# A hybrid decoder layer on one core: weights laid out in the order of their use, and loaded in longer runs and larger chunks

## The reference, cut to what matters

```
proj = xn @ w_in                      # 1024 x 11264, then w_a, w_b, w_o
...
logits = xt @ w_router ; top 4 of 32 experts per token, gates = softmax(top)
h = xb @ w1[e] + b1[e]                # 1024 x 2048 per expert
gate = min(h[:, :1024], 7) ; up = clip(h[:, 1024:], -7, 7)
y = ((up + 1) * gate * sigmoid(1.702 * gate)) @ w2[e] + b2[e]   # 1024 x 1024
```

## Time and profile before

| what | value |
|---|---|
| three runs | 1490.82, 1487.87, 1491.01 us; median 1490.82 |
| the profiled execution | span 1490.0 us, 0.8 us below the median; the page gives no time beyond the span |
| TensorE matmuls busy | 1384.2 us, 93% |
| VectorE, ScalarE, GpSimd busy | 25%, 15%, 6% |
| bytes moved | 518.50 MB (10^6 bytes), mean 348 GB/s over the span |
| loads of the ring | SP's queue, 469.10 MB |

### The profile page before, as it was taken

The page is one execution under the profiler, slowest core; times in us unless marked ns, Lnnn a source line. Parts: engine busy times, 40 slices in busy tenths (PEclk is TensorE's granted clock), DMA queues, the critical chain, the costliest instruction groups (busy, mean ns, idle before and its releaser), DMA issues.

```text
span 1490.0 us, 18645 instructions
## 1 busy us (share of the span) xinstructions
PE 1384.2 (93%) x7365; PEld 705.1 (47%) x7365; DVE 374.4 (25%) x677; ACT 228.6 (15%) x340; POOL 96.3 (6%) x160
## 2 busy tenths in 40 slices
PE   7999999999999998998999989989999899899896
PEld 6667668778887433333333333333323333333231
DVE  3224332532501322122122121221221212211123
ACT  1122232211000411111001011110110111110102
POOL 1022222210000200000000000000000000000000
PEclk9999999999999999999999999999999999999999
DMA  9887868876334479999999999999999999999995
GB/s 351 311 292 282 282 238 292 273 252 208 135 134 175 165 290 420 415 420 417 415 422 415 418 420 415 420 416 416 421 415 419 418 415 422 415 417 420 415 420 214
DMA packets 119137, 518.50 MB, mean 348 GB/s; under 512 B 9240, under 2 KB 9512, under 8 KB 86303
## 3 DMA queue, kind: packets, MB, share of 16 engines
q1 hardware_dynamic: 104442, 469.10, 78.4%
q0 software_dynamic: 12720, 45.14, 9.0%
q10 hardware_dynamic: 1940, 3.78, 0.7%
HBM read 496.35 MB, written 21.67 MB: 348 GB/s over the span
## 4 chain that ended last, share of the span: by engine, by line
PE 76%; DMA 12%; SPq 4%; DVE 3%; ACT 2%; issue 1%; POOL 0%; DVEq 0%; ACTq 0%; POOLq 0%
PE bank L1522 25%; PE bank L1258 18%; PE bank L1557 11%; PE bank L1568 6%; DMA ring<-in_w_e 6%; SPq L520 4%; DMA out_ret_sample<-arena 4%; PE bank L1502 3%; PE bank L1301 3%; PE bank L1395 2%; PE bank L1520 1%; ACT arena L848 1%; PE bank L1360 1%; DVE arena L1209 1%; DVE hx L1213 1%
## 5 line engine op out<-in xcount | busy, mean ns | idle before, releaser
L1522 PE MATMUL bank<-ring,arena 128*64 128x512 f32 x2048 | 444.8, 592 | 0.3 <-ACT arena L839 0.3
L1258 PE MATMUL bank<-arena,ring 128*128 128x264 f32 x1536 | 350.3, 388 | 0.0
L1258 PEld LDWEIGHTS bank<-arena,ring 128*128 128x128 f32 x1536 | 290.2, 190 | 53.4 <-issue 5.0
L1522 PEld LDWEIGHTS bank<-ring,arena 128*64 128x64 f32 x2048 | 143.8, 137 | 283.3 <-issue 277.8
L1557 PE MATMUL bank<-ring,arena 128*64 128x512 f32 x1024 | 227.2, 593 | 5.0 <-DMA ring<-in_w_e 5.0
L1557 PEld LDWEIGHTS bank<-ring,arena 128*64 128x64 f32 x1024 | 70.9, 137 | 139.9 <-issue 117.5
L1198 DVE TENSOR_SCALAR arena<-bank 128x512 f32<-128x512 f32 x32 | 22.1, 692 | 397.0 <-PE bank L1522 397.0
L1568 PE MATMUL bank<-arena 128*128 128x512 f32 (+1 forms) x192 | 91.3, 610 | 12.6 <-DVE arena L1209 12.6
L1502 PE MATMUL bank<-arena 128*128 128x128 bf16 x768 | 60.0, 236 | 29.6 <-DVE arena L1190 29.5
L1209 DVE COPY arena<-bank 64x512 f32<-64x512 f32 x32 | 21.9, 683 | 236.1 <-PE bank L1557 236.1
L1502 PEld LDWEIGHTS bank<-arena 128*128 128x128 bf16 x768 | 54.6, 107 | 44.7 <-issue 44.7
(11 more groups left out here) (198 smaller groups left out, 819.3 us busy)
## 6 DMA issues: line engine op xcount, KB each, us to landing
ring<-in_w_e SPq DMA_DIRECT2D x384, 1024.0 KB, 18.4
ring<-in_w_in SPq DMA_DIRECT2D x44, 1024.0 KB, 12.8
arena<-in_state_ret POOLq DMA_DIRECT2D x32, 512.0 KB, 6.3
out_ret_sample<-arena POOLq DMA_DIRECT2D x32, 512.0 KB, 5.8
arena<-v_decode POOLq DMA_DIRECT2D x32, 256.0 KB, 7.9
ring<-in_w_b SPq DMA_DIRECT2D x8, 1024.0 KB, 7.2
ring<-in_w_a SPq DMA_DIRECT2D x4, 1024.0 KB, 12.8
ring<-in_w_o SPq DMA_DIRECT2D x4, 1024.0 KB, 6.1
```

Source lines behind the costliest of these rows:

```text
L1258: ins = pe.matmul(bank[:, 0:T], weight(n + k // 4, k % 4)[:, 128 * j:128 * (j + 1)], rhs[:, k, :], start=k == 0, stop=k == KD * groups - 1)
L1522: ins = pe.matmul(out, xgT[:, k, 64 * e:64 * (e + 1)], ring[:, (KD * e + k) % RING, c:c + 512], start=False, stop=k == KD - 1)
```

## The change

The host hands over the weights as two new arrays. `w_mixer` holds the mixer's 60 chunks in order of use, each with its 128 partitions' 2048 floats contiguous (runs of 8 KB). `w_pairs` holds for each pair of experts 6 chunks of 4 MB (four of `w_e1`, with four of the eight row blocks each, and two of `w_e2`), each with 8192 contiguous floats for a partition (runs of 32 KB). For the experts the ring becomes 3 slots of 4 MB (`WIDE_SLOTS`), each over four of the old slots (`SLOT_CHUNKS`), with the first one's semaphore. The bytes, the matmuls and their order stay as they are. The laying out is done before the launch and is in no measured time.

```
+W1_CHUNKS = 2
+W2_CHUNKS = W1_CHUNKS // 2
+W1_KS, W2_FS = KD // W1_CHUNKS, KD // W2_CHUNKS
+PAIR_CHUNKS = 2 * (W1_CHUNKS + W2_CHUNKS)
+WIDE = W1_KS * 2 * D
+WIDE_SLOTS = RING * CH // WIDE
+SLOT_CHUNKS = RING // WIDE_SLOTS
...
+def laid_out_mixer(inputs):
+
+    parts = [inputs[name][0, row:row + 512, c:c + 512].reshape(4, 128, 512).transpose(1, 0, 2)
+             for name, row, c, _ in mixer_parts()]
+    return np.ascontiguousarray(np.stack(parts)).reshape(MIXER_CHUNKS, 128, CH)
+
+
+def laid_out_experts(inputs):
+
+    w1 = np.asarray(inputs["w_e1"][0]).reshape(PAIRS, 2 * W1_CHUNKS, W1_KS, 128, 2 * D).transpose(0, 1, 3, 2, 4)
+    w2 = np.asarray(inputs["w_e2"][0]).reshape(PAIRS, 2 * W2_CHUNKS, W2_FS, 128, D).transpose(0, 1, 3, 2, 4)
+    out = np.empty((PAIRS, PAIR_CHUNKS, 128, WIDE), np.float32)
+    out[:, :2 * W1_CHUNKS].reshape(w1.shape)[...] = w1
+    out[:, 2 * W1_CHUNKS:].reshape(w2.shape)[...] = w2
+    return out
...
-                sp.dma_start(ring[:, n % RING, :].rearrange("p (k n) -> p k n", k=4), src).then_inc(chunk[n % RING], 16)
+                sp.dma_start(ring[:, n % RING, :], w_mixer[n]).then_inc(chunk[n % RING], 16)
...
+                for n in range(PAIR_CHUNKS):
+                    at = SLOT_CHUNKS * (n % WIDE_SLOTS)
+                    dst = ring[:, at:at + SLOT_CHUNKS, :].rearrange("p a n -> p (a n)")
+                    src = w_pairs[bass.ds(pair, 1), n].rearrange("o p n -> p (o n)")
+                    if n >= WIDE_SLOTS:
+                        used(it, n - WIDE_SLOTS)
+                    elif first:
+                        for part in range(SLOT_CHUNKS):
+                            slot_free(MIXER_CHUNKS - RING + at + part)
                     else:
-                        used(it - 1, n + RING)
-                    sp.dma_start(dst, src).then_inc(chunk[n % RING], 16)
+                        used(it - 1, n + PAIR_CHUNKS - WIDE_SLOTS)
+                    sp.dma_start(dst, src).then_inc(chunk[at], 16)
...
-                            if k >= 0:
-                                slot_ready(KD * e + k)
+                            n = W1_CHUNKS * e + k // W1_KS
+                            if k >= 0 and k % W1_KS == 0:
+                                slot_ready(n)
...
-                            if k >= 0:
+                            if k >= 0 and k % W1_KS == W1_KS - 1:
                                 ins.then_inc(up_done if k == KD - 1 else chunk_used, 1)
...
-                            n = 2 * KD + 4 * e + f // 2
-                            if f % 2 == 0:
+                            n = 2 * W1_CHUNKS + W2_CHUNKS * e + f // W2_FS
+                            if f % W2_FS == 0:
                                 slot_ready(n)
...
-                            if f % 2 == 1:
+                            if f % W2_FS == W2_FS - 1:
                                 ins.then_inc(down_done if f == KD - 1 else chunk_used, 1)
```

More of the change, by code:

```diff
@@ L104, in shape_constants, with mixer_parts, columns @@
     return c
+def mixer_parts():
+    def columns(name, row, c, last):
+        return [(name, row + 512 * half, c, last) for half in range(2)]
+    for g in range(2):
+        yield from columns("w_in", 0, W_Q + 512 * g, ("proj", ("q", g), 3))
+        yield from columns("w_in", 0, W_K + 512 * g, ("proj", ("k", g), 3))
+        for h in (2 * g, 2 * g + 1):
+            yield from columns("w_in", 0, W_V + DV * h, ("v", h, 1))
+            yield from columns("w_in", 0, W_G + DV * h, ("proj", ("g", h), 3))
+    w_conv = dict(cc=W_CC, ch=W_CH, cb=W_CB)
+    for n, g in CONV_ORDER:
+        yield from columns("w_in", 0, w_conv[n] + 512 * g, ("proj", (n, g), 3))
+    yield from columns("w_in", 0, W_GA, ("proj", ("ga", 0), 3))
+    yield from columns("w_in", 0, W_CB + 512, ("proj", ("cb", 1), 3))
+    yield from columns("w_in", 0, W_GA + 512, ("proj", ("ga", 1), 3))
+    for n, w, c in (("wa", "w_a", 0), ("gb", "w_in", W_GB)):
+        for g in range(2):
+            yield from columns(w, 0, c + 512 * g, ("proj", (n, g), 3))
+    for g in range(2):
+        for half in range(2):
+            yield from columns("w_b", D * half, 512 * g, ("proj", ("wb", g), 3))
+    for g in range(2):
+        yield from columns("w_o", 0, 512 * g, ("wo", 1, g))
+def laid_out_mixer(inputs):
[9 more added lines that the diff above has]
+    return out
 PROJ_BANKS = 3
@@ L421, in was_filled @@
             eng.wait_ge(filled[bank], n)
[L423 to L459, removed]
+        w_mixer, w_pairs = a["w_mixer"], a["w_pairs"]
         @block.sync
@@ L476, in _ @@
             sp.dma_start(prow[R_NORM2:R_NORM2 + 1, :], a["norm2"]).then_inc(prow_in, 16)
-            mixer = list(mixer_chunks())
+            mixer = [last for *_, last in mixer_parts()]
             assert len(mixer) == MIXER_CHUNKS
             def slot_free(n):
-                was_filled(sp, mixer[n][1])
-            for n, (src, _) in enumerate(mixer):
+                was_filled(sp, mixer[n])
+            for n in range(MIXER_CHUNKS):
                 if n >= RING:
                     slot_free(n - RING)
-                sp.dma_start(ring[:, n % RING, :].rearrange("p (k n) -> p k n", k=4), src).then_inc(chunk[n % RING], 16)
+                sp.dma_start(ring[:, n % RING, :], w_mixer[n]).then_inc(chunk[n % RING], 16)
@@ L506, in load_pair @@
-            def load_pair(it, pair, first=False):
[L507 to L510, removed]
-                    else:
[L512 to L518, removed]
-                        used(it - 1, n + RING)
-                    sp.dma_start(dst, src).then_inc(chunk[n % RING], 16)
+                if n < 2 * W1_CHUNKS:
+                    e, part = divmod(n, W1_CHUNKS)
+                    if part == W1_CHUNKS - 1:
+                        sp.wait_ge(up_done, 2 * it + (e + 1 + PRIMED))
+                    else:
+                        sp.wait_ge(chunk_used, COUNTED * it + ((W1_CHUNKS - 1) * e + part + 1))
+                else:
+                    e, part = divmod(n - 2 * W1_CHUNKS, W2_CHUNKS)
+                    if part == W2_CHUNKS - 1:
+                        sp.wait_ge(down_done, 2 * it + (e + 1))
+                    else:
+                        sp.wait_ge(chunk_used, COUNTED * it + (2 * (W1_CHUNKS - 1) + (W2_CHUNKS - 1) * e + part + 1))
@@ L1490, in slot_ready, with held @@
                     def slot_ready(n):
-                        pe.wait_ge(chunk[n % RING], 32 * it + 16 * (uses_before + n // RING + 1))
+                        uses = PAIR_CHUNKS // WIDE_SLOTS
+                        pe.wait_ge(chunk[SLOT_CHUNKS * (n % WIDE_SLOTS)],
+                                   16 * uses * it + 16 * (uses_before + n // WIDE_SLOTS + 1))
+                    def held(n, at):
+                        at += SLOT_CHUNKS * CH * (n % WIDE_SLOTS)
+                        return ring[:, at // CH, at % CH:at % CH + 512]
                     pe.wait_ge(P_ready, 2 * it + (1 + PRIMED))
@@ L1522, in _ @@
                                         ins = pe.matmul(out, xgT[:, k, 64 * e:64 * (e + 1)],
-                                                        ring[:, (KD * e + k) % RING, c:c + 512], start=False, stop=k == KD - 1)
-                            if k >= 0:
+                                                        held(n, 2 * D * (k % W1_KS) + c), start=False, stop=k == KD - 1)
+                            if k >= 0 and k % W1_KS == W1_KS - 1:
                                 ins.then_inc(up_done if k == KD - 1 else chunk_used, 1)
@@ L1569, in _ @@
                                       start=True, stop=True).then_inc(combined, 1)
-INPUTS = ["x_prompt", "x_sample", "state_conv", "state_ret", "norm1", "w_in", "conv_w", "w_a", "w_b", "w_o", "norm2",
-          "w_router", "b_router", "w_e1", "b_e1", "w_e2", "b_e2", "norm_f"]
+INPUTS = ["x_prompt", "x_sample", "state_conv", "state_ret", "norm1", "conv_w", "norm2",
+          "w_router", "b_router", "b_e1", "b_e2", "norm_f"]
 OUTPUTS = [("y_prompt", (1, LP, D)), ("y_sample", (NS, 1, D)), ("conv_prompt", (1, 1, 2, D)),
@@ L1584 @@
     arrays["tables"] = shape_constants()
+    arrays["w_mixer"] = laid_out_mixer(inputs)
+    arrays["w_pairs"] = laid_out_experts(inputs)
     a = {n: nc.dram_tensor(f"in_{n}", x.shape, F32, kind="ExternalInput").ap() for n, x in arrays.items()}
```

11 lines of the change are left out of this document (1 added, 10 removed).

## The result

The changed kernel takes 1498.67 us (median of 16 runs, 1490.37 to 1505.89) against 1490.27 (16 runs of the kernel before): ratio 1.0056, 95% interval 1.0045 to 1.0067. It is **8.4 us slower**; 1484 was forecast, within 1479 to 1497. The profiled execution has a span of 1497.3 us, 7.3 more than before.

The account below looks back on a forecast made before the run. TensorE was taken to bound the mixer, with transfers and TensorE close together in the expert stage. Issues 0, mixer 0, first chunks 0 and waits for loads -7.2 us took 1490.8 to 1483.6, stated as 1484, range 1479 to 1497.

Parts of the forecast that it names:

- the slack of the sixth chunk: Expert pairs: sixth chunk lands 38.65 us after the pair's start, TensorE wants it at 39.49; 0.84 us spare, 0.4 at 422 GB/s.
- In a stage that TensorE bounds, it costs nothing as long as each load lands in time: Expert stage: the larger chunks' coarser grain costs nothing if TensorE is the bound; 10.4 us once if transfers are.
- the fourth load: Expert pairs: first load on the path to the sixth chunk, 2.3 us start-up, then 4.19 MB at 428 GB/s.
- Rival B: Expert pairs: three slots are too few, a stall in each pair, 1502 us; decides from 1.3 us extra latency; chance 0.10.
- Longer runs for the mixer. I take 0: Mixer: 8 KB runs for ring loads win at best 4.5 us, with rival C against it; taken as 0.
- Rival C: Mixer: state transfers wait behind 8 KB ring packets, up to 13 us on their chain, 1497 us; chance 0.08.
- The rate: Expert loads: runs of 32 KB move at 426 to 431 GB/s, taken as 428.
- The estimate of 426: Expert loads: by the skill's fixed cost of about three bus cycles a packet, 422 GB/s would become 426.
- 424.8 GB/s is enough: Expert stage: at this rate 390.07 MB of refills land in 918.3 us, so loads finish in time.
- the 7.2 us: Expert stage: TensorE's waits for loads, 7.18 us of the excess, go away; the whole forecast gain.
- The clock of the gathers: Between expert pairs: five of 15 gathers run slow, expected five again, give or take one; none or ten means 8 us.

Follow-up runs that it names:

- e6_split4: The changed kernel with the mixer's old loads (2 KB runs) and each pair's fourth 4 MB load issued in four 1 MB quarters: 1484.24 us against 1490.39.
- e1_mixer_only: The kernel before with only the mixer's weights laid out in order of use (8 KB runs), experts as before: 1493.91 us against 1490.57.
- e7_mixer_2kb: The kernel before with the mixer's chunks contiguous and in order of use, but again in 2 KB runs: 1490.08 us against 1490.39.
- e3_grain: The changed kernel with old mixer loads and three 4 MB expert slots filled from the old arrays in old runs (8 and 4 KB): 1512.86 us against 1490.57.
- e8_mixer_hold: As e1_mixer_only, but SP holds back ring loads after the two kept heads' value projections until the kept values' stores land: 1491.48 us against 1490.39.
- e5_1mb: The changed kernel with the mixer's old loads and the experts in twelve 1 MB slots, all 8 KB runs: 1482.95 us against 1490.39.
- e4_2mb: The changed kernel with the mixer's old loads and the experts in six 2 MB slots, 16 KB runs: 1482.72 us against 1490.57.

## Why the prediction was wrong

**The step that failed is the slack of the sixth chunk** ("The slack is 0.84 us", "at 422 it is 0.4"), and with it the sentence "In a stage that TensorE bounds, it costs nothing as long as each load lands in time". The term that was mis-sized is the fourth load: 2.3 us of start-up and 9.8 of transfer, 12.1 in all. The 2.3 was taken from a 1 MB load that found the engines idle and carried over to one of 4 MB. Measured, that load takes 12.2 to 14.7 us and a queued one 9.7, so that 2.5 to 5.0 us come on top. On engines that were really idle, in the first pair, it is 13.8, 4.1 on top. In the other pairs the term was not even of the right kind, by the prediction's own numbers: three loads of 9.8 us behind the sixth chunk's 38.65 end at 68.05, 9.4 us into the next pair, whereas the fourth load is issued at 6.95. What lies on top there is partly the rest of the load in progress and partly time lost between the two; why that loss is 0 in one pair and 2.7 us in another stays open.

Rival B named the place and the point of decision, 1.3 us of extra latency, and was given 1 in 10. In the profile it came to a late fifth or sixth chunk in nine of 16 pairs, and cost 4.3 us over the stage before, not 19; `e6_split4` shows that with this one load in quarters nearly the whole gain appears (6.2 us).

**The clock's answer to a wait was not in any price.** A wait of 0.3 us in front of a `w_e2` product came with 1.75 us more in the product itself (8.78 against 7.03, at a granted clock of 0.81). It did so after two of the ten waits (743.35 and 1043.52), both at the fifth chunk; after the others, of up to 0.9 us, the product took 7.09. I had counted the clock only for the gathers.

**"Longer runs for the mixer. I take 0" failed too**, by 3.3 us (`e1_mixer_only`). Rival C had the mechanism, a transfer of another queue that waits behind 8 KB packets, and looked at the states' chain alone. What reached TensorE first was the store of the kept values, of which the earlier trace rows showed TensorE's wait already (2.2 us, the longest of the mixer). A wait with no slack at all passes on each added microsecond, and here the products behind it can lose more by the clock than the wait itself grew. `e7_mixer_2kb` against `e1_mixer_only` shows by the times that the length of runs is the cause. For the place the profiles are weaker evidence: the store lands after 10.7 to 12.3 us and the wait is 2.9 to 4.6 us in the three with 8 KB runs, and 9.7 to 10.7 and 1.9 to 3.0 in the eight with 2 KB runs (`e3_grain` has the 10.7 and 3.0). With the store out of the way the cost appeared, in the one profile of `e8_mixer_hold`, at the states, where the rival had put it. The rule of the Trainium skill cited there (DMA: Bandwidth & Descriptors, Queues, rings and completion order) goes with what was seen; that packets alternate one by one no row shows.

**The rate was right in sign and on the low side.** 426 to 431 GB/s were expected. Over 40 us of queued loads the profile after has

```profile
560.00:600.00 40.00, 34.62 (x192) 13.11 (x190) 9.94 (x15) 4.78 (x7) 0.49 (x2) 1.00 1.00 433
```

With 433 for 428 the path would be 0.3 us shorter; that was less than the fourth load's error. The estimate of 426 that rests on the Trainium skill (DMA: Bandwidth & Descriptors, Why small descriptors are slow) is lower still.

**"424.8 GB/s is enough" and the 7.2 us were right** for the bytes, not for this grain. The finer grain needs even less (420.1): `e5_1mb` runs at 422 without a wait and is 7.4 us faster than before.

**The clock of the gathers**: five slow ones again, as expected. The routing differs between executions by its clock as well. The last `w_o` product took 5.33 us in the profile after, and 3.68 before; `e1_mixer_only`, with the mixer loads of the change, has 3.68 too, and `e5_1mb`, with those of before, has 5.38. Of the 3.0 us by which the pairs start later, 1.65 are this, and it isn't the change's. The start of the pairs varies anyway: in the eight profiles with 2 KB runs in the mixer it lies between 528.6 and 532.5 us, so that the mixer's loss rests on the times of `e1_mixer_only` and `e7_mixer_2kb`.

In sum: -7.2 (waits for loads) + 0 (mixer) was expected; the halves measured are +3.9 (experts) and +3.3 (mixer). The expert part missed by 11 us, which a finer grain gives back.

## What to carry to other kernels

A ring of few large slots is judged by the first load that is issued when no other is left in the queue: its release, its own time and the loads behind it are one chain against the consumer's path. That load's time varied by 2.5 us within one execution here, so a slack below that should be read as a stall, the more so where a short wait can also cost TensorE its clock. Longer runs pay by their rate, so lengthen them only until the consumer is the bound (here 8 KB), and keep the grain fine. Longer packets in one queue are paid by other queues: look for transfers that an engine already waits for, however short the wait, and for those next in line, before giving the bulk loads longer runs.

## What was not expected of the hardware

A load of 4 MB that is issued while the engines are idle, or while only the last microseconds of another are left, takes 12.2 to 14.7 us in one and the same execution, and queued ones 9.7. In the completion records of the trace (16 for each load) the 16 engines' completions of such a load lie 0.6 to 3.0 us apart in the profile after; the spread stays the same through the loads queued behind it and is a new one at each fourth load. In the kernel before, whose queue never empties in the pairs, it is 1.6 to 1.9 us from the first refills to the last. The spread alone costs nothing: in `e6_split4`, where TensorE waits for no load, it reaches 3.4 us. Why it is drawn anew wasn't tried.

Run lengths of 4, 8, 16 and 32 KB gave, with loads queued, 410, 422, about 430 and 433 GB/s; for 16 KB the row is `e4_2mb` from 600 to 640 us:

```profile
DMA packets 1178, 17.20 MB, mean 430 GB/s; under 512 B 128, under 2 KB 128, under 8 KB 128
```
